# Sample attention moved into the blocks of the prompt attention, with a second, transposed copy of the cache

## The reference, cut to what matters

```
prompt:  k_nope, v = ckv @ w_uk, ckv @ w_uv                     (8 heads, 1024 keys, causal, blocks of 128 queries)
         softmax((q_nope.k_nope + q_pe.kpe) * SCALE) @ v
sample:  q_abs = q_nope @ w_uk^T                                (32 query rows x 8 heads)
         softmax((q_abs.ckv_all + q_pe.kpe_all) * SCALE) @ ckv_all @ w_uv
         ckv_all, kpe_all = 2048 cached rows (16 pages of 128, found by page_table) + the 4 new rows
conv:    c = depthwise conv, width 31, over 512 channels, then LayerNorm and swish
out:     h = h + concat(attention, c) @ w_o
```

## Time and profile before

| | |
|---|---|
| median of 3 runs | 2477.78 us (2474.61 to 2484.24) |
| the profiled execution | 2484.98 us, its span 2483.2 us |
| busy in the span | PE 2314.1 us, DVE 1351.2, ACT 632.7, GpSimd 388.6 |
| mean granted TensorE clock | 0.959 of full speed |
| DMA | 123.01 MB, 50 GB/s over the span |

### The profile page before, as it was taken

One profiled execution on the slowest core, in us unless ns is written; L12 is line 12 of the kernel. 1 busy time (PEld: TensorE's weight loads), 2 busy tenths in 40 slices (PEclk: granted clock), 3 DMA queues, 4 the chain that ended last, 5 costly groups with the idle time before them and its releaser, 6 DMA issues.

```text
span 2483.2 us, 36895 instructions
## 1 busy us (share of the span) xinstructions
PE 2314.1 (93%) x14466; PEld 2146.1 (86%) x14466; DVE 1351.2 (54%) x2071; ACT 632.7 (25%) x1043; POOL 388.6 (16%) x248
## 2 busy tenths in 40 slices
PE   6999999999998998788877879999999999999896
PEld 6999999999998997455444559999999999999896
DVE  6444444444446642887688973644444444444746
ACT  5211111111113241333332342311111111112523
POOL 0000000000000001999999100000000000000000
PEclk9999999999999999788879989999999999999998
DMA  4111111111111104000013511111111111111201
GB/s 142 49 45 42 42 42 51 34 51 51 51 51 34 51 26 51 14 14 13 0 47 102 163 54 37 51 52 51 42 43 50 37 48 50 35 51 51 67 27 70
DMA packets 53998, 123.01 MB, mean 50 GB/s; under 512 B 9985, under 2 KB 30882, under 8 KB 53730
## 3 DMA queue, kind: packets, MB, share of 16 engines
q1 hardware_dynamic: 47730, 112.92, 15.4%
q10 hardware_dynamic: 5264, 5.67, 0.8%
q0 software_dynamic: 928, 3.38, 0.4%
HBM read 115.85 MB, written 6.09 MB: 49 GB/s over the span
## 4 chain that ended last, share of the span: by engine, by line
PE 79%; DVE 11%; ACT 4%; issue 3%; DMA 1%; SPq 1%; ACTq 0%; DVEq 0%
PE ps L426 24%; PE ps L428 23%; PE ps L427 23%; PE ps L587 4%; DVE cacc L1593 2%; PE ps L612 1%; PE ps L602 1%; ACT pr L1047 1%; DVE cacc L1511 1%; DVE cacc L1509 1%; PE ps L744 1%; DMA raw<-in_wstream 1%; DVE rstd L1209 1%; DVE q L1527 1%; ACT sq L810 1%
## 5 line engine op out<-in xcount | busy, mean ns | idle before, releaser
L426 PE MATMUL ps<-n_hi,wlo 128*128 128x352 f32 x2832 | 924.6, 326 | 27.2 <-DVE wlo L1192 11.7
L428 PE MATMUL ps<-n_hi,whi 128*128 128x352 f32 x2832 | 914.4, 323 | 0.0
L427 PE MATMUL ps<-n_lo,whi 128*128 128x352 f32 x2832 | 913.1, 322 | 0.0
L426 PEld LDWEIGHTS ps<-n_hi,wlo 128*128 128x128 f32 x2832 | 535.5, 189 | 31.3 <-DVE wlo L1192 12.6
L427 PEld LDWEIGHTS ps<-n_lo,whi 128*128 128x128 f32 x2832 | 537.0, 190 | 2.1 <-issue 0.2
L428 PEld LDWEIGHTS ps<-n_hi,whi 128*128 128x128 f32 x2832 | 536.1, 189 | 0.0
L1257 DVE TENSOR_TENSOR gu<-ps,rstd 128x704 f32<-128x704 f32 x132 | 117.6, 891 | 506.8 <-PE ps L428 506.8
L426 PE MATMUL ps<-hid_hi,wlo 128*128 128x352 f32 x1104 | 360.9, 327 | 18.5 <-DVE h L1239 18.3
L428 PE MATMUL ps<-hid_hi,whi 128*128 128x352 f32 x1104 | 356.7, 323 | 0.0
L427 PE MATMUL ps<-hid_lo,whi 128*128 128x352 f32 x1104 | 356.2, 323 | 0.0
L1239 DVE SCALAR_TENSOR_TENSOR h<-ps,h 128x352 f32<-128x352 f32 x552 | 273.7, 520 | 150.4 <-PE ps L428 149.2
(11 more groups left out here) (181 smaller groups left out, 1854.4 us busy)
## 6 DMA issues: line engine op xcount, KB each, us to landing
raw<-in_wstream SPq DMA_DIRECT2D x167, 512.0 KB, 3.6
ctile<-in_cache SPq DMA_DIRECT2D x100, 144.0 KB, 2.4
ctile<-in_cache ACTq DMA_DIRECT2D x28, 144.0 KB, 2.7
pw<-in_pairw SPq DMA_DIRECT2D x4, 800.0 KB, 4.4
h<-in_xT SPq DMA_DIRECT2D x2, 1408.0 KB, 9.8
out_yT<-n POOLq DMA_DIRECT2D x2, 1408.0 KB, 6.2
h<-in_xT ACTq DMA_DIRECT2D x4, 352.0 KB, 5.4
out_ckvT<-ckv SPq DMA_DIRECT2D x1, 1056.0 KB, 9.1
```

Of the source, the lines that this page charges most:

```text
L426: nc.tensor.matmul(out, w_l, x_h, start=first, stop=False)
L427: nc.tensor.matmul(out, w_h, x_l, start=False, stop=False)
L428: return nc.tensor.matmul(out, w_h, x_h, start=False, stop=last)
```

## The change

The sample attention is cut into 40 slots, ten for each pair of heads, and spread over the 32 blocks of the prompt attention. The loop over pairs is written out.

- **Cache.** The host passes the cache twice: `cacheT`, transposed (96 x 3 x 128 for each page, latents and rotary key), for the scores, and `cache` (128 x 256, latents alone) for the values. The transposes L637 and copies L305 go. There are 32 loads of eight pages, all issued by SP, into two buffers in turn. Scores are kept whole in `SS`, so that one maximum and one exponential in four parts take the place of the running softmax.
- **Slots.** S: scores of 256 tokens. N: the new tokens. T and U: transposes of probabilities. V: values of 256 tokens. W: values of the new tokens. O: transposes of the output. Pairs 0 and 2 hold the eight S, N and the first T; pairs 1 and 3 hold the eight V with the T's, then W and O.
- **Residual.** `h` is written to DRAM (`hsave`) by GpSimd while the input projection runs. Its space holds the cache buffers, the rotated queries and weights. It is read back in three parts, which `add_tile` of the output projection waits for.
- **Projections.** The rotary parts of all heads, the sample's queries and the first pair's projections are computed during the last four GLU tiles (`prologue(8)` to `prologue(11)`); those of a later pair after the transposes of block 7 of the pair before. GpSimd copies the rotated queries into `q`.
- **Softmax.** PE adds the causal mask (a matmul of `ident` and `tri`). ACT scales the second head's probabilities and does all copies to `PT`.
- **Convolution.** DVE does all 124 taps: 8 ahead of the first block and 29 for each pair, as `TAPS_AT` says. GpSimd does none.

```diff
+TAPS_AT = (1, 2, 2, 2, 3, 3, 4, 12)
+def sample_slots():
+    slots = []
+    for g in range(2):
+        slots += [[("S", g, c)] for c in range(TILES)]
+        slots += [[("N", g, 0)], [("T", g, 0)]]
+        slots += [[("V", g, c), ("T", g, c + 1)] for c in range(TILES - 1)]
+        slots += [[("V", g, TILES - 1), ("U", g, 0)], [("W", g, 0)], [("O", g, 0)]]
+    return slots
+for _n, _slot in enumerate(SLOTS):
+    _pair, _k = divmod(_n, len(SLOTS) // PAIRS)
+    SLOTS_AT.setdefault(QB * _pair + (0, 0, 1, 1, 2, 3, 4, 5, 6, 7)[_k], []).append(_slot)
...
@@ load_tile(eng, n)
+        kind, g, c = C_ORDER[n]
+        if n >= 2:
+            before = C_ORDER[n - 2]
+            if before[0] == "S":
+                eng.wait_ge(b_ready, B_ORDER.index(before) + 1)
+            else:
+                eng.wait_ge(c_used, TILES * before[1] + before[2] + 1)
+        for j in range(4):
             for pg in range(PPT):
                 page = eng.value_load(ptab[0:1, at:at + 1], min_val=0, max_val=cache.shape[0] - 1)
+                if kind == "S":
+                    eng.dma_start(tT[n % 2][:, j, pg, :, :], cacheT[page]).then_inc(c_in[n % 2], 16)
+                else:
+                    eng.dma_start(tN[n % 2][:, j, pg, :], cache[page]).then_inc(c_in[n % 2], 16)
@@ sync: convp and convs are issued here, ahead of the loads
+        for n in range(LOADS):
+            if n == 0:
+                sp.wait_ge(rope_done, GROUPS4)
+            if n == 1:
+                sp.wait_ge(proj_ready, Z_PRO)
...
+            load_tile(sp, n)
+        sp.wait_ge(c_used, 2 * TILES)
+        sp.wait_ge(q_rope, HEADS)
+        h_reload(0)
+        sp.wait_ge(s_ready, UNITS)
         for s in range(RAW):
             sp.dma_start(raw[(N_WO + s) % RAW][:, :], wstream[N_WO + s]).then_inc(raw_in[(N_WO + s) % RAW], 16)
+        h_reload(1)
+        h_reload(2)
@@ tensor
+            for s in range(STEPS):
+                p, i = block_of(s)
+                ends = i == QB - 1
+                if not ends:
+                    scores(s + 1)
...
+                for op in slots[0]:
+                    sample_step(*op)
+                if i:
+                    values(s - 1)
+                for slot in slots[1:]:
+                    for op in slot:
+                        sample_step(*op)
+                transposes(s)
+                if ends and p < PAIRS - 1:
...
+                    for r in range(NRB):
+                        pair_tile(p + 1, r, r, nope_tile, w, PW_NOPE, r)
+                    pair_tile(p + 1, 3, 3, uk_tile, w, 0)
+                    pair_tile(p + 1, 4, 0, uk_tile, w, 1)
+                if ends:
+                    values(s)
+                if ends and p < PAIRS - 1:
+                    pair_tile(p + 1, 5, 1, uv_tile, w, 0)
+                    pair_tile(p + 1, 6, 2, uv_tile, w, 1)
+                    pe.wait_ge(proj_free, proj_count(p + 1, Z_PAIR))
+                    pe.wait_ge(q_rope, 2 * (p + 2))
+                    scores(s + 1)
@@ scalar
+        for s in range(STEPS):
+            p, i = block_of(s)
+            exponentials(s)
+            if i:
+                transposed_out(s - 1)
+            scale_second(s)
+            for slot in SLOTS_AT[s]:
+                for op in slot:
+                    sample_step(*op)
+            if i:
+                high_av(s - 1)
+            if i == QB - 1:
+                transposed_out(s)
...
@@ vector
+        convolve(len(taps) - PAIRS * sum(TAPS_AT))
+        for s in range(STEPS):
+            p, i = block_of(s)
+            peaks(s)
+            convolve(1)
+            step.hit(inverse(s, 0))
+            step.sync()
+            scale_first(s)
+            inverse(s, 1).then_inc(s_recip, 1)
+            for slot in SLOTS_AT[s]:
+                for op in slot:
+                    sample_step(*op)
+            more = TAPS_AT[i] - 1
+            convolve(min(2, more))
+            if i:
+                low_av(s - 1)
+            convolve(more - min(2, more))
+            if i == QB - 1:
+                low_av(s)
```

More of the change, by code:

```diff
@@ L509, in latent_sum, with project, nope_tile @@
             row_sum(Y_WIN + WIN_ORDER.index(f"l{x}"), lat_red, x + 1, sqs[:, 0, :])
+        def project(out, w, col, width, chunks, rhs):
+            for c in range(chunks):
+                last = nc.tensor.matmul(out, w[:, col + c * width:col + (c + 1) * width], rhs(c), start=(c == 0),
+                                        stop=(c == chunks - 1))
+            return last
+        def nope_tile(bank, w, col, r):
+            n = RB if r < NRB - 1 else SEQ - r * RB
+            return project(ps[:, bank, 0:n], w, col, P, QC, lambda c: cq[:, c, r * RB:r * RB + n])
@@ new lines, in uk_tile, with uv_tile @@
+        def uk_tile(bank, w, half):
+            return project(ps[:, bank, :], w, PW_UK, P, VC, lambda c: ckv[:, c, 512 * half:512 * (half + 1)])
+        def uv_tile(bank, w, half):
+            for i in range(4):
+                s0 = (4 * half + i) * P
+                for c in range(VC):
+                    last = nc.tensor.matmul(ps[:, bank, i * P:(i + 1) * P], ckv[:, c, s0:s0 + P],
+                                            w[:, PW_UV + c * P:PW_UV + (c + 1) * P], start=(c == 0), stop=(c == VC - 1))
+            return last
@@ new lines, in sample_absorb @@
+        def sample_absorb(bank, hh):
+            for p in range(PAIRS):
+                for c in range(C96):
+                    m = min(K96, KV_RANK - c * K96)
+                    w0 = p * KV_RANK + c * K96
+                    at = (p * C96 + c) * NEW
+                    last = nc.tensor.matmul(ps[0:m, bank, at:at + NEW], ukT[NOPE * hh:NOPE * (hh + 1), w0:w0 + m],
+                                            qn[NOPE * hh:NOPE * (hh + 1), p * NEW:(p + 1) * NEW], start=True, stop=True)
+            return last
@@ new lines, in values @@
+        def values(s):
+            p, i = block_of(s)
+            pe.wait_ge(t_done, T_ORDER.index(("P", 2 * s + 1, i // 4 * 4)) + 1)
+            if s:
+                pe.wait_ge(av_lo, s)
+            for j in range(i + 1):
+                for hh in range(2):
+                    last = nc.tensor.matmul(ps[VH * hh:VH * (hh + 1), 6, 0:P], V[:, j, VH * hh:VH * (hh + 1)],
+                                            PT[:, s % 2, hh, j * P:(j + 1) * P], start=(j == 0), stop=(j == i))
+            last.then_inc(av_ready, 1)
@@ L738, in _ @@
-        pe.wait_ge(av_lo, 2 + PAIRS * QB + 1)
+                prologue(x)
+        attention()
         def ln_sums(m):
@@ L1576, in _ @@
[L1576 to L1583 removed]
+            if x == 6:
+                rope_keys()
+            if x == 8:
+                new_latents()
+            if x in (9, 10):
+                rope_queries(x - 9)
+        taps = [(c, x) for half in range(2) for x in range(TAPS) for c in (2 * half, 2 * half + 1)]
```

1056 lines of the change are left out of this document (495 added, 561 removed).

## The result

The kernel after takes 2501.39 us (median of 5 runs, 2497.85 to 2505.55), the kernel before 2477.78 (5 runs, 2472.31 to 2484.24): ratio 1.0086, 95% interval 1.0067 to 1.0105, 0.9% slower. The forecast was 2500.

A forecast was written before the change was run, and what follows sets the result against it. Neither PE nor DVE is full in a pair; the chain of waits decides. Start 1006.5 plus four pairs and closing product gave 1479.5 against 1453.8; less 3 for early weights, profiled 2508, median 2500 us, range 2420 to 2570.

The forecast's parts named there:

- The loop: Within a pair: page issue (8.7 us a load) sets early blocks, DVE's and ACT's order later ones; S pair 111.5 us.
- the signs: Expected in the trace: page issues 1.09 us apart, PE's longest idles ended by loads (blocks 0-2) and exponentials (3-6).
- Rival 1: In the pairs, waits overlap better, periods 8.7 us or less in blocks 2 to 5: 95 us a pair, 2422; chance 0.22.
- Ahead of block 0: From the GLU tiles' end: 26 us of PE products, then eight taps on DVE; block 0's maximum at 1006.5.
- The term for `convs`: On SP's queue before the cache loads: four issues taking 10.26 us, so the first load starts at 1006.4.
- The first pair's surplus: In the first pair: waiting for its own loads, not there in advance, adds 16 us.
- S and V pairs: Pairs with S slots 111.5 us, with V slots 105 because DVE doesn't wait; clock adds 8 and 5.
- The clock: PE's clock near 0.75 in the pairs, low in blocks 1 to 4: 8 us an S pair, 5 a V pair.
- After the attention: Behind attention: the output projection's first weights are already there, saving perhaps 3 us.
- The sum: End of attention at 1479.5 against 1453.8, 26 us later; profiled execution 2508, median 2500 us, +0.9%.
- Rival 2: In the pairs, the clock stays up because slots bring many short matmuls: 26 us of clock terms go, 2475; chance 0.20.
- Rival 3: The clock stays down in all blocks because PE waits for loads: about 100 us more, 2600; chance 0.13.

The follow-up runs named there:

- experiment 1: Kernel after with each page number a constant instead of a word read from the page table (wrong pages, same loads): 2459.46 us, 1.7% below the kernel after.
- experiment 5: Kernel after with SP reading a load's eight page numbers before it waits for the buffer: 2492.69 us, 0.4% below the kernel after.
- experiment 8: Kernel after with a pair's ten slots in blocks 0, 1, 2, 3, 4, 5, 5, 6, 6, 7: 2462.09 us, 1.6% below the kernel after.
- experiment 2: Kernel after with ScalarE copying the previous block's transposed probabilities ahead of the exponentials: 2478.23 us, 0.9% below the kernel after.
- experiment 4: Kernel after with one tap in each block, 84 of 124 taps left out: 2468.21 us, 1.4% below the kernel after.
- experiment 6: Kernel after with the slot's maximum and the values' split put behind the next block's maxima on VectorE: 2469.25 us, 1.3% below the kernel after.
- experiment 9: Kernel after with up to two further taps of each block ahead of its sample steps on VectorE: 2479.96 us, 0.8% below the kernel after.
- experiment 11: Kernel after with four edits together, those of experiments 2, 5, 8 and 9: 2405.54 us, ratio 0.9709 against the kernel before.
- experiment 12: Experiment 11 with half of each load's pages issued by GpSimd; the fastest version with nothing left out: 2385.15 us, 3.7% below the kernel before.
- experiment 7: Kernel after with 2 or 4 extra matmuls on PE ahead of its waits for loads 2 to 5 of each eight: 2519.54 us, 0.7% slower.

## Why the prediction was right, step by step

**The loop.** Right in mechanism, with one shift. Issue sets block 1 (experiments 1, 5 and 8), and not blocks 0 to 2: the second load of block 1 is used 23.3 us after the third pair's start where 24 stood, and block 2 hardly changes with cheap issues. The strict lists of DVE and ScalarE set blocks 2 to 6 (2, 4, 6 and 9), and block 7 is 27.8 us where 27 stood, on PE's side. Of PE's waits in the third pair, those for loads stand in block 1 alone (3.7 and 5.5 us). Those for an exponential, 1.5 to 2.6 us, stand in blocks 1 to 4, and the longest of all, 5.5, 5.5 and 7.5 us in blocks 5 to 7, are for ScalarE's copies of the transposes, which I had in the loop but not among the signs. The forecast had pairs of 135.5, 110, 119.5 and 108 (the last with its closing product); they came at 129.7, 109.4, 119.2 and 104.3. Rival 1 failed for the reason given against it: the lists are strict. Once the lists and the issue were mended, the pairs came near its 95 us: 87 to 107 in experiments 11 and 12. Its own sign, periods of 8.7 us or less, then holds in blocks 2 to 4 of the third pair (6.3, 7.2 and 8.5 us in experiment 11) and not in block 5 (16.3).

**Ahead of block 0.** 1005.3 against 1006.5. The closeness is partly luck: eight taps at the forecast's own 1.35 us are 10.8, from 994 to 1004.8 and not 1006.5; they took 10.0 and began 1.3 later. And in the kernels of the experiments, which change nothing ahead of block 0, its maximum begins between 1001.5 and 1006.0. The term for `convs` was wrong: 3.71 us, not the 10.26 of the earlier trace rows. The DMA engines moved 240 GB/s in that stretch (974.3 to 984.6), here 76 (996.2 to 999.9). The first load began at 1000.99 and not at 1006.4.

**The first pair's surplus** was forecast at 16 us, all for loads, and is 10.5 over the third pair. Its cause is only in part the one forecast. The kernel without slots has no loads, and its first pair is still 6.7 us longer than its third (85.1 and 78.4), 5.4 of it in block 0. What I had left out is that ScalarE's list has the copies of the absorbed queries (1005.90 to 1008.41), one more copy and a table load of 1.28 us ahead of block 0's exponential, which ran at 1010.12, 4.8 us after the maximum (5.7 in the kernel without slots):

```profile
1008.82 1.28 ACT L1119 ACT_TABLE_LOAD   x1
1010.12 0.37 ACT L1119 ACTIVATE pr<-ps,stat 128x128 f32<-128x128 f32 x1
```

**S and V pairs.** The difference between them was forecast at 9.5 and measured at 9.8 us. It is DVE's order, as experiment 9 shows by taking it away. The forecast had 6.5 for that order and 3 for the clock, so the order was worth more than it said and the agreement of the whole is partly luck.

**The clock.** Forecast "near 0.75", measured 0.72, 0.88, 0.77 and 0.82. It was forecast low in blocks 1 to 4; in the third pair it is low in blocks 1 and 2 (0.54 and 0.65), back at 1.00 and 0.86 in blocks 3 and 4, and 0.77 and 0.78 in 5 and 6. Its price of 8 and 5 us is not confirmed: experiment 7 did not raise the clock on the chain, and no experiment separates the clock from the list orders. The S pair without a clock term, 111.5 us, is 7.7 short of the 119.2 measured, as much as the 8 us added, but that is no proof of the term: 5.5 of these 7.7 lie between the second slot of block 1 and the last S (45.5 us where 40 stood), where the order of the lists costs time as well. What the rows do give is PE's busy time for the same 14198 instructions: 2268.6 us in the kernel after (mean clock 0.948), 2241.4 in the fastest version (0.973). The lower clock costs at least some of that 27 us; how much of it is on the chain they don't say.

**After the attention.** The 3 us for the early weights did not show: 39.60 us in both, and 0.5 us more to the end of the span.

**The sum.** The terms were off by -1.2 ahead, -5.8, -0.6, -0.3 and -3.7 in the pairs, and +3 behind: the profiled execution was forecast 23 us above that of before and is 14.6 above. The median is 23.6 above, since the profiled execution of before lay 7.2 above its median and that of after 1.8 below. The hit on 1.4 us is therefore partly luck; on the traces alone the forecast was 8 us too slow.

**Rivals.** Rival 2 (clock stays up): out, 0.72 to 0.88. Rival 3 (clock stays down in all blocks): out, four of eight blocks of the third pair have 0.83 or more.

Taking the slots out gives 151 us; the orders and the issue together give 95 (2499.6 to 2404.8 in the profiled executions), and 114 with GpSimd. PE's own work on the slots is enough to account for the rest. The fastest version is 36.6 us slower than the kernel without slots, and its PE is busy 46.4 us more (2241.4 and 2195.0). So what the slots still cost there is less than PE's time for them; in the kernel after it was twice that time (151.0 and 73.6).

What stays open is how much of blocks 1 to 6 is the clock.

## What to carry to other kernels

Work put into the waits of a loop costs its full time, or more, if every engine's list puts it between two links of the loop's chain. Here a separate stage of 139 us, which held 40 taps as well, became 151 us inside, about 74 of them PE's own time and the rest waits. So before moving work in, write each engine's list beside the chain and place the new steps where that engine waits, not where it is about to be waited for: four edits of place and order, without a change of the arithmetic, turned +0.9% into -2.9%. And count the issue of many register-addressed DMAs as work on one queue: where loads bunch up, spread them, or use a second, idle engine.

## What the runs showed of the hardware

- **Issue cost.** A page with its register read takes SP 1.09 us (1.07 in the kernel after), one with a constant address 0.53, one with the number read earlier 0.45. The Trainium skill ("DMA: Bandwidth & Descriptors", section "Issuing engines are not separate DMA queues") calls the sequencer time that several issuing engines save usually small; here a page lands 2.2 us after its issue and issuing it takes half as long, the register reads alone were worth 1.7% of the kernel, and a second engine 0.8%.
- **GpSimd's issues** took 0.57 us a page and landed in 3.9 us, where SP's in the same kernel landed in 3.4 (2.6 when SP issued alone in the kernel with four edits, 2.2 in the kernel after). VectorE's taps were not slower beside them: 1281 ns on average against 1277 in the kernel with four edits.

```profile
tT<-in_cacheT POOLq DMA_DIRECT2D x64, 144.0 KB, 3.9
tT<-in_cacheT SPq DMA_DIRECT2D x64, 144.0 KB, 3.4
```

- **The same issue can cost 3.71 or 10.26 us** for four, in a stretch of 76 and one of 240 GB/s; that the traffic is the cause was not tested. A duration from one place of a trace is at most a bound at another.
- **A block's mean clock is not the clock on its chain.** In experiment 7, in a block with a mean of 0.78, a slot took 1.50 us behind a wait of 0.25 us and 2.79 behind one of 4.11; only the second is on the chain.
